# A hybrid mixer and mixture-of-experts layer: the last stage fetches both expert outputs of 64 tokens onto the two halves of the partitions and sums them with two column tiles

## The chip, the core and the metric

The kernel runs on one core of a Trainium2 chip. The metric is the device time in microseconds (us) of one execution. The profile shows one execution; its span runs from the first to the last instruction of the program.

## What is computed

The reference runs one decoder layer on 1,088 tokens of width 1,024 (1,024 of a prompt, 64 of eight samples): four token mixers, an output projection, and a mixture of experts, in which each token picks two of 32 experts. A final RMSNorm gives the output. The part that matters here is the end:

```python
w2 = jax.nn.softmax(v2, axis=-1) * p_top          # two gates of each token
...
out = jnp.einsum('nef,efd->nd', act, w_down)      # gated sum of the two experts' outputs
...
x = x + hier_moe(...)
...
y = rmsnorm(x, g_final)
```

## The kernel before

Tokens stand in nine tiles of 128 rows (the last, tile 8, has 64). The experts run in 28 blocks (`step`); each block gathers its tokens, multiplies, and scatters its ungated output rows into a scratch tensor in HBM, `orow`, where token n has the two rows 2n and 2n+1, one for each choice. Weights of later blocks are loaded meanwhile by the SP queue, in order.

On VectorE (DVE) small pieces of table work hang behind certain blocks, in a dictionary `between` (keys 1 to 10 before). Once the last block is scattered, GpSimd (POOL) raises `moe_done`, and the last stage begins:

- SP issues nine loads at L732, in the order `FINAL = [8, 0, 1, 2, 3, 4, 7, 5, 6]`. Each brings the two output rows of a token, 8 KB that lie together, onto that token's own partition (`opair`). Behind them the same queue issues the nine stores of the result (L559), in the same order, each when `y_done` says so.
- Tiles of `PE_TILES` (0, 2, 4, 5, 6) are summed by TensorE (PE): `own_rows(t)` (L2600) copies x into a pair of PSUM banks by the identity, and four products (L2617) add the choices, with the gates on the diagonals of `dg` as weights. There are four pairs of banks, so the fifth tile waits for the DVE to be done with the first. ScalarE (ACT) builds the ten diagonals at L1169 as soon as the gates are there.
- Tiles of `DVE_TILES` (8, 1, 3, 7) are summed by DVE in two instructions each (`add_experts`, L2082).
- ACT squares and sums each tile and takes the root (L1176 or L749, L1161); DVE inverts it and scales (`final_norm`, L2090 and L2095); SP stores.

The gates are computed by DVE after the last block (L2067 to L2071) and released by `gates_ready`, which PE also uses to know that DVE has left the banks of the last blocks.

Some blocks have two or four experts at a time. There `expert_D` and `expert_GU` write products of 64 or 32 output columns to different partitions of one bank, so that the array is split into column tiles (L2545 and L2506).

Of the kernel before, what the change touches and what calls it, by code (L numbers as in the profile page):

```python
# [23 lines left out]
ALU = mybir.AluOpType  # L24
ACT = mybir.ActivationFunctionType
AX_X = mybir.AxisListType.X

P = 128
D = 1024
# [5 lines left out]
TILES = NT // P + 1  # L35
# [4 lines left out]
NE, NG, EG, FF = 32, 4, 8, 128  # L40
# [30 lines left out]
SPARE = 3  # L71
XG = 4
FINAL = [8, 0, 1, 2, 3, 4, 7, 5, 6]
PE_TILES = [0, 2, 4, 5, 6]
DVE_TILES = [8, 1, 3, 7]
NPAR = 31 + 3 + 4


# [135 lines left out]
def rows(i):  # L214

    return NS if i == LAST else P


def build_layer(nc, a):
    with ExitStack() as ctx:  # L220
        def sb(name, shape, dt=F32):
            return ctx.enter_context(nc.sbuf_tensor("sb_" + name, shape, dt))
# [10 lines left out]
        o_x1 = o_ring + 4 * D * 4  # L233
# [7 lines left out]
        def at(name, shape, offset, dt=F32):  # L241
            return nc.alloc_sbuf_tensor_at("at_" + name, shape, dt, offset=lo + offset)
# [43 lines left out]
        def opair(i):  # L286
            return opair_s[:] if i == LAST else opair_p[:, i, :]
# [18 lines left out]
        ovm = at("ovm", [1, NE], o_sg + 3328)  # L306
        again = at("again", [1, NE + 1], o_w + 14624)
        ovb = at("ovb", [1, 3, OVER], o_sg + 3456)
        dg = at("dg", [P, len(PE_TILES), 2, P], o_x1 + 2 * D * 4)
        xin = at("xin", [P, TILES, D], o_x1)  # L310
        x1 = at("x1", [P, TILES, D], o_mix)
        wk = at("wk", [P, 3, WL], o_w)
# [23 lines left out]
        ident = sb("ident", [P, P])  # L336
        ones = sb("ones", [P, P])
        avg = sb("avg", [P, P])
# [39 lines left out]
        sc = sb("sc", [P, 8])  # L378
        gidx = sb("gidx", [P, 1])
        gates = sb("gates", [P, TILES, 2])  # L380
# [3 lines left out]
        carry = sb("carry", [P, NE])  # L384
        rank = sb("rank", [P, NE])
        rjunk = sb("rjunk", [P, NE])
        rk = sb("rk", [P, 2])
        stage = sb("stage", [P, 3, W])
        rki = sb("rki", [P, 2], I32)
# [6 lines left out]
        gex = flat[:, TILES * 56:TILES * 61].rearrange("p (t n) -> p t n", t=TILES)  # L396
        gsum = flat[:, TILES * 61:TILES * 62]
# [11 lines left out]
        orow = nc.dram_tensor("scratch_out", [2 * NT, D], F32, kind="Internal").ap()  # L409

        s = {n: sem(n) for n in (
            "dve_chain", "act_chain", "pool_chain",
            "const_ready", "ident_ready", "gcol_ready", "scol_ready", "zero_ready",
            "small_in", "ws_in", "late_in", "gain_mix_in", "gain_mix_ready", "ln_d_in",
            "gain_ffn_in", "gain_fin_in", "pw_in", "wsT_masked", "wsb_in",
            "sq_done", "rs_ready", "h_ready", "ht_T", "ht_hi", "ht_lo",
            "hi_ready", "lo_ready", "piece_done", "zf_act", "zf_dve",
            "m_ready", "mf_act", "mf_dve", "uc_ready", "v_stats", "v_rsd",
            "v_ready", "v_out", "px_ready", "pd_ready", "ac_ready", "ua_ready",
# [3 lines left out]
            "t2_done", "h2T_ready", "last_T", "last_h2T", "rows_in", "pads_ready", "gex_in", "gex_out", "m_onehot",  # L423
            "eid_ready", "perm_ready", "ones_ready", "place_ready", "table_added", "cols_ready", "idx_ready", "ov_ready", "xg_zero", "three_gathers",
            "xt_half", "xt_done", "first_hi", "first_lo", "htm_hi", "htm_lo", "w_hi0", "w_hi1", "w_lo0", "w_lo1", "gu_half", "gu_done", "sg_ready", "act_ready", "at_done", "att_ready",
            "d_done", "ob_act", "ob_dve", "moe_done", "gates_ready", "dg_ready", "pair_summed", "y_sum", "y_root", "y_done", "y_out")}
        x_in = [sem(f"x_in{i}") for i in range(TILES)]
        raw_in = [sem(f"raw_in{i}") for i in range(2)]
        wo_in = [sem(f"w_out_in{n}") for n in range(3)]
# [5 lines left out]
        pair_in = [sem(f"pair_in{i}") for i in range(TILES)]  # L435
# [113 lines left out]
        def sum_banks(t):  # L549
            return ps[:, t % 4 * 2:t % 4 * 2 + 2, :]  # L550
# [14 lines left out]
        def _(sp):  # L565
# [58 lines left out]
            for g in range(4):  # L624
                q = g % 2 * 64
# [57 lines left out]
            for i in range(TILES):  # L683
# [6 lines left out]
                if i in (4, 7):  # L690
                    n = i // 3 - 1
# [14 lines left out]
            for w in range(FIX, NE):  # L706
                c = LOADS[w - FIX]
# [20 lines left out]
            sp.wait_ge(s["moe_done"], 1)  # L728
            for i in FINAL:
                n = rows(i)  # L730
                src = orow[2 * i * P:2 * (i * P + n), :].rearrange("(t k) d -> t (k d)", k=2)
                sp.dma_start(opair(i)[0:n, :], src).then_inc(pair_in[i], 16)  # L732
            for at in range(TILES):
# [8 lines left out]
        def _(act):  # L742
            do = Chain(act, s["act_chain"])
            A = nc.scalar.activation
# [84 lines left out]
            for i in range(TILES):  # L829
                n = rows(i)  # L830
# [333 lines left out]

            act.wait_ge(s["gates_ready"], 1)
            for t, i in enumerate(PE_TILES):
                n = rows(i)
                for k in range(2):
                    do(A(dg[0:n, t, k, 0:n], ident[0:n, 0:n], ACT.Copy, scale=gates[0:n, i, k:k + 1]),  # L1169
                       s["dg_ready"])  # L1170
            do(A(acts[:], epsc[:], ACT.Sqrt))
            for i in FINAL:
                if i in PE_TILES:
                    t = PE_TILES.index(i)
                    act.wait_ge(s["pair_summed"], t + 1)
# [198 lines left out]
        def _(dve):  # L1374
            do = Chain(dve, s["dve_chain"])
            v = nc.vector
            stt, tt, ts = v.scalar_tensor_tensor, v.tensor_tensor, v.tensor_scalar
# [41 lines left out]
            for c in range(2):  # L1419
                for h in range(2):  # L1420
                    q = slice(h * 64, h * 64 + 64)
# [52 lines left out]
            for i in range(TILES):  # L1474
                n = rows(i)
                do(v.bn_stats(st6[0:n, i, :], vall[0:n, i, :]))
            for i in range(TILES):
                n = rows(i)
# [5 lines left out]
            for i in range(TILES):  # L1484
                n = rows(i)
# [535 lines left out]
            def overflow_blocks():  # L2021
# [3 lines left out]
                do(v.tensor_copy(ovt[:, OVER:2 * OVER], ovb[:, 2, :]))  # L2025
                do(v.tensor_copy(ovt[:, 2 * OVER:2 * OVER + 1], incl[:, NE - 1:NE]), s["ov_ready"])

            between = {1: expert_order, 2: light_columns, 3: extra_columns, 4: other_columns,
                       6: overflow_counts, 7: overflow_sums, 8: overflow_lists, 9: overflow_experts,
                       10: overflow_blocks}  # L2030

# [31 lines left out]
                                expert_out(i, r, bank=0)  # L2063


            dve.wait_ge(s["gex_out"], 1)
            do(v.tensor_reduce(gsum[:], gex[:, :, 0:NG], AX_X, ALU.add))  # L2067
            do(ts(gates[:, :, 0], gex[:, :, NG], 1.0, None, ALU.add))
            do(tt(gates[:, :, 0], gates[:, :, 0], gsum[:], ALU.mult))
            do(v.reciprocal(gates[:, :, 0], gates[:, :, 0]))  # L2070
            do(tt(gates[:, :, 1], gates[:, :, 0], gex[:, :, NG], ALU.mult), s["gates_ready"])  # L2071


            dve.wait_ge(s["moe_done"], 1)
            dve.wait_ge(s["gain_fin_in"], 16)
            def add_experts(i):

                n = rows(i)
                dve.wait_ge(pair_in[i], 16)
                dve.wait_ge(x_in[i], 48)  # L2080
                for k in range(2):
                    do(stt(x1[0:n, i, :], opair(i)[0:n, k * D:(k + 1) * D],  # L2082
                           gates[0:n, i, k:k + 1], x1[0:n, i, :], ALU.mult, ALU.add),
                       s["y_sum"] if k == 1 else None)
# [16 lines left out]
            final_norm(1)  # L2101
            final_norm(2)
            add_experts(3)
            add_experts(7)
            final_norm(3)
            final_norm(4)
            final_norm(7)
# [5 lines left out]
        def _(pe):  # L2113
# [23 lines left out]
            for h, b in ((0, 6), (1, 7)):  # L2137
                mm = pe.matmul(ps[:, b, :], ones[0:1, :], gain[0:1, h * 512:h * 512 + 512],
                               start=True, stop=True)
# [75 lines left out]
            for c in range(2):  # L2215
                mm = pe.transpose(b[:, c * 64:c * 64 + NPAR], par_rows[0:NPAR, c * P:(c + 1) * P],
                                  ident[0:NPAR, 0:NPAR])
            mm.then_inc(s["m_ready"], 1)
            b = m_open("stc")
            for c in range(2):  # L2220
                for h in range(2):
                    q = (2 * c + h) * 120
                    mm = pe.transpose(b[:, q:q + 120], st_rows[0:120, h, c * P:(c + 1) * P],
                                      ident[0:120, 0:120])
# [3 lines left out]
            for r, n, q in ((2, SB * HP, 0), (3, SB * HA, 240)):  # L2228
                for c in range(2):
                    mm = pe.transpose(b[:, q + c * n:q + (c + 1) * n], st_rows[0:n, r, c * P:(c + 1) * P],  # L2230
                                      ident[0:n, 0:n])
# [3 lines left out]
            for h in range(NG):  # L2235
                mm = pe.transpose(b[:, h * P:(h + 1) * P], ws_rows[:, h, :], ident[:])
# [6 lines left out]
            for i in range(TILES):  # L2243
                n = rows(i)
                b = m_open(f"v{i}")
                for k in range(KC):
                    for hpart, wpart in ((0, 0), (0, 1), (1, 0)):
                        mm = pe.matmul(b[0:n, 0:W].rearrange("p (s c) -> p s c", s=2),  # L2248
                                       hT[:, hpart, k, i * P:i * P + n],
                                       vw[:, :, wpart, k * P:(k + 1) * P],  # L2250
                                       start=(k, hpart, wpart) == (0, 0, 0),
                                       stop=(k, hpart, wpart) == (KC - 1, 1, 0))
# [342 lines left out]
            def own_rows(t):  # L2595

                i = PE_TILES[t]
                pe.wait_ge(x_in[i], 48)
                for h in range(2):
                    pe.matmul(sum_banks(t)[:, h, :], ident[:], x1[:, i, h * 512:(h + 1) * 512],  # L2600
                              start=True, stop=False)

            own_rows(1)
            pe.wait_ge(s["gates_ready"], 1)
            pe.wait_ge(s["dg_ready"], 1)
            for t in (0, 2, 3):
                own_rows(t)
            for t, i in enumerate(PE_TILES):
                if t == 3:
                    pe.wait_ge(s["y_done"], FINAL.index(PE_TILES[0]) + 1)  # L2610
                    own_rows(4)
                pe.wait_ge(pair_in[i], 16)
                pe.wait_ge(s["dg_ready"], 2 * t + 2)
                for h in range(2):
                    for k in range(2):
                        q = k * D + h * 512
                        mm = pe.matmul(sum_banks(t)[:, h, :], dg[:, t, k, :], opair(i)[:, q:q + 512],  # L2617
                                       start=False, stop=k == 1)
                mm.then_inc(s["pair_summed"], 1)


# [29 lines left out]
```

## Time and profile before

| What | us |
|---|---|
| Median of 3 runs | 603.12 (602.17 to 603.79) |
| Profiled execution: its own time | 600.14 |
| Profiled execution: span | 598.4 |
| PE busy in the span | 564.5 (94%) |
| DVE busy | 437.8 (73%) |
| ACT busy | 240.2 (40%) |

The granted clock of the profiled execution is 0.982 of TensorE's full speed on average. The busy shares are averages over stages with different limits; the change touches the last stage, about the last 36 us, and two places in the middle of the expert blocks.

### The profile page before, as it was taken

The page shows a single profiled execution, that of the slowest core. Times are in us where ns is not written, and L with a number is a line of the kernel's source. Part 1 is how long each engine was busy: PE and PEld are TensorE (multiplying, and loading weights), DVE is VectorE, ACT ScalarE, POOL GpSimd, SP SyncE. Part 2 cuts the span into 40 slices and gives each one's busy share as a digit, 9 for nine tenths or more (in the row PEclk, how much of TensorE's full clock was granted, in tenths as well). Part 3 has the DMA queues.
Part 4 walks back from the last instruction along what each step waited for, and adds up shares of the span by engine and source line. Part 5 has one row for each costly group of instructions (what it writes and reads, how often), then busy time and mean ns, then how long its engine had stood idle before and what let it go on. Part 6 is the DMA issues. An engine that isn't in the chain of part 4 may idle for free.

```text
span 598.4 us, 9751 instructions
## 1 busy us (share of the span) xinstructions
PE 564.5 (94%) x3392; PEld 467.9 (78%) x3392; DVE 437.8 (73%) x748; ACT 240.2 (40%) x385; POOL 87.1 (15%) x138
## 2 busy tenths in 40 slices
PE   8899999999999999899999997699999999998685
PEld 6799999998899889788888875588766667885232
DVE  4946997999999976835666658889864457875177
ACT  6752112222122425522222114577444447765434
POOL 4400000200000000000000000422533333521100
PEclk9999999999999999999999999799999999999798
DMA  8751210122010320475525337759999999998599
GB/s 307 157 132 40 70 36 1 36 61 68 19 54 17 135 71 1 142 256 211 211 106 222 130 110 244 247 146 378 409 409 409 388 369 390 403 357 315 185 421 370
DMA packets 54773, 120.16 MB, mean 201 GB/s; under 512 B 10867, under 2 KB 29176, under 8 KB 53625
## 3 DMA queue, kind: packets, MB, share of 16 engines
q1 hardware_dynamic: 47237, 101.10, 47.0%
q0 software_dynamic: 6880, 17.84, 8.3%
q8 instruction: 29, 0.48, 0.3%
q10 hardware_dynamic: 596, 0.50, 0.3%
q14 instruction: 31, 0.25, 0.1%
HBM read 100.29 MB, written 25.80 MB: 211 GB/s over the span
## 4 chain that ended last, share of the span: by engine, by line
PE 39%; DVE 18%; SPq 9%; DMA 9%; issue 3%; ACT 2%; POOL 0%; POOLq 0%; DVEq 0%; ACTq 0%
PE ps L2380 14%; PE ps L2202 9%; SPq L650 8%; DMA at_wlater<-in_expert_w_down 4%; DVE at_mixP L1444 3%; DMA at_opair_p<-scratch_out 2%; PE ps L2545 2%; PE ps L2444 2%; DMA scratch_out<-at_outb,at_sperm 2%; PE ps L2506 2%; PE ps L2617 2%; DVE at_hT L1403 1%; PE ps L2485 1%; DVE at_lnsq L1630 1%; PE ps L2130 1%
## 5 line engine op out<-in xcount | busy, mean ns | idle before, releaser
L2202 PE MATMUL ps<-at_hT,at_ring 128*128 128x384 f32 x936 | 165.5, 333 | 0.0
L2202 PEld LDWEIGHTS ps<-at_hT,at_ring 128*128 128x128 f32 x936 | 155.9, 188 | 5.1 <-issue 5.0
L2380 PE MATMUL ps<-at_hT,at_mring 128*128 128x512 f32 (+1 forms) x432 | 102.7, 393 | 1.9 <-DVE at_mring L1598 1.3
L2380 PEld LDWEIGHTS ps<-at_hT,at_mring 128*128 128x128 f32 (+1 forms) x432 | 77.3, 182 | 21.3 <-DVE at_mring L1598 1.7
L1444 DVE SCALAR_TENSOR_TENSOR at_mixP<-at_uc,at_par,at_mixP 128x1024 f32<-128x1024 f32 x60 | 77.1, 1285 | 2.1
L2520 PE MATMUL ps<-at_whi,at_hTm 128*128 128x256 f32 x176 | 50.8, 289 | 0.0
L2522 PE MATMUL ps<-at_whi,at_hTm_lo 128*128 128x256 f32 x176 | 49.3, 280 | 0.0
L2485 PEld LDWEIGHTS ps<-sb_ident,at_xg 128*128 128x128 f32 x224 | 28.3, 191 | 17.6 <-issue 14.5
L749 ACT ACTIVATE at_wk<-at_x 128x1024 f32<-128x1024 f32 (+1 forms) x13 | 13.8, 1059 | 50.6 <-DVE at_x L1670 44.8
L1886 DVE TENSOR_TENSOR at_hTm_lo<-ps,at_hTm 128x1024 fp32r<-128x1024 f32 x21 | 25.7, 1223 | 10.4 <-ACT at_hTm L1049 10.3
L2520 PEld LDWEIGHTS ps<-at_whi,at_hTm 128*128 128x128 f32 x176 | 33.1, 188 | 0.1
L2522 PEld LDWEIGHTS ps<-at_whi,at_hTm_lo 128*128 128x128 f32 x176 | 33.1, 188 | 0.0
L2485 PE MATMUL ps<-sb_ident,at_xg 128*128 128x128 f32 x224 | 30.4, 279 | 2.6 <-DMA at_xg<-scratch_h,at_gidxs 2.4
L1301 POOL DMA_INDIRECT scratch_out<-at_outb,at_sperm x20 | 19.8, 988 | 68.6 <-DVE at_outb L1874 68.6
L1874 DVE COPY at_outb<-ps 128x512 f32<-128x512 f32 x28 | 19.2, 686 | 13.8 <-PE ps L2545 6.4
L1904 DVE TENSOR_TENSOR at_wfirst_lo<-at_wfirst,at_whi 128x1024 fp32r<-128x1024 f32 x18 | 22.1, 1225 | 8.5 <-ACT at_whi L1068 8.1
L1092 ACT ACTIVATE at_outb<-ps 128x512 f32<-128x512 f32 x28 | 16.7, 598 | 27.2 <-PE ps L2545 17.3
L1286 POOL DMA_INDIRECT at_xg<-scratch_h,at_gperm x20 | 23.2, 1161 | 20.1 <-issue 13.6
L2248 PE MATMUL ps<-at_ring,at_hT 128*128 128x256 f32 (+1 forms) x216 | 25.9, 282 | 0.0
L2248 PEld LDWEIGHTS ps<-at_ring,at_hT 128*128 128x128 f32 (+1 forms) x216 | 25.8, 185 | 0.0
L2545 PE MATMUL ps<-at_wlater,at_actT 128*128 128x512 f32 (+1 forms) x60 | 23.0, 601 | 2.0 <-ACT at_actT L1083 2.0
L1049 ACT ACTIVATE at_hTm<-ps 128x1024 fp32r<-128x1024 f32 x21 | 21.6, 1026 | 7.3 <-PE ps L2485 7.3
(331 smaller groups left out, 955.3 us busy)
## 6 DMA issues: line engine op xcount, KB each, us to landing
at_raw<-in_w_in SPq DMA_DIRECT2D x16, 512.0 KB, 3.9
at_opair_p<-scratch_out SPq DMA_DIRECT2D x8, 1024.0 KB, 13.9
at_wlater<-in_expert_w_gate SPq DMA_DIRECT2D x15, 512.0 KB, 13.1
at_wlater<-in_expert_w_up SPq DMA_DIRECT2D x15, 512.0 KB, 16.4
at_wlater<-in_expert_w_down SPq DMA_DIRECT2D x15, 512.0 KB, 20.6
at_wfirst<-in_expert_w_gate SPq DMA_DIRECT2D x9, 512.0 KB, 11.3
at_wfirst<-in_expert_w_up SPq DMA_DIRECT2D x9, 512.0 KB, 13.8
at_wfirst<-in_expert_w_down SPq DMA_DIRECT2D x9, 512.0 KB, 16.0
```

What stands on the lines that cost most here:

```text
L650: sp.dma_start(wexp(j)[:, m * D:(m + 1) * D], src)\
L1286: g.indirect_dma_start(xg[0:n, b % XG, :], None, hs, bass.IndirectOffsetOnAxis(ap=index[0:n, :], axis=0), bounds_check=last_token, oob_is_ ...
L1444: do(stt(y, x, par[:, c, k:k + 1], y, ALU.mult, ALU.add))
L1886: v.tensor_tensor(hTm_lo[j % 2][:], src, hTm[:, j % 2, :, :].bitcast(F32), ALU.subtract).then_inc(s["htm_lo"], 1)
L1904: v.tensor_tensor(half(wexp_lo(w), h), half(wexp(w), h), whi[h][:].bitcast(F32), ALU.subtract).then_inc(s[f"w_lo{h}"], 1)
L2202: mm = pe.matmul(ps[:, bank + r, 0:t1 - t0], w[:, wpart, k * P:(k + 1) * P], hT[:, hpart, k, t0:t1], start=(m, wpart, hpart) == (0, 0, 0), ...
L2248: mm = pe.matmul(b[0:n, 0:W].rearrange("p (s c) -> p s c", s=2), hT[:, hpart, k, i * P:i * P + n], vw[:, :, wpart, k * P:(k + 1) * P], sta ...
L2380: mm = pe.matmul(ps[0:n, b + r, :], mring[:, 1 - i % 2, mpart, k * P:k * P + n], wo[:, wpart, k, r * 512:(r + 1) * 512], start=(c, mpart, ...
L2485: mm = pe.transpose(rows_psum(b)[:, k // 4, k % 4 * P:(k % 4 + 1) * P], xg[:, j % XG, :].rearrange("p (q k) -> p k q", k=KC)[:, k, :], ide ...
L2520: pe.matmul(out, x, high, start=k == 0, stop=False)
L2522: mm = pe.matmul(out, x_low, high, start=False, stop=k == KC - 1)
L2545: mm = pe.matmul(ps[n, bank + r, :], actT[:, j % 2, n], wexp(w)[:, q:q + 512], start=True, stop=True)
```

## The change

For the six tiles of `PE_TILES` (tile 7 joins them and leaves DVE) the load is made in two pieces. The first choices of the tile's tokens, in two groups of 64 tokens, go to partitions 0 to 63, and the second choices to partitions 64 to 127; a partition holds one row of a token of the first group and one of the second. One piece is 64 partitions by two rows of 4 KB. A weight matrix of 128 by 64, with the first gates on one diagonal and the second gates on the other below it, then sums both choices of 64 tokens in one product; the two groups of tokens go to the two halves of the output partitions.

The gates are computed behind block 12 and laid out in the new form behind block 14. A tiny copy on DVE, `dve_clear`, takes over what `gates_ready` told PE. With six tiles on four pairs of banks, two of them wait for a `y_done`.

```diff
-PE_TILES = [0, 2, 4, 5, 6]
-DVE_TILES = [8, 1, 3, 7]
+PE_TILES = [0, 2, 4, 7, 5, 6]
+DVE_TILES = [8, 1, 3]
...
-        dg = at("dg", [P, len(PE_TILES), 2, P], o_x1 + 2 * D * 4)
+        dg = at("dg", [P, len(PE_TILES), 2, P // 2], o_x1 + 2 * D * 4)
...
+        gates2 = rjunk[:, 0:2 * TILES].rearrange("p (t h) -> p t h", t=TILES)
+        ident2 = avg[:, 0:P // 2]
...
             for i in FINAL:
                 n = rows(i)
+                if i in PE_TILES:
+                    src = orow[2 * i * P:2 * (i + 1) * P, :].rearrange("(h t k) d -> k t h d", h=2, k=2)
+                    for k in range(2):
+                        sp.dma_start(opair(i)[64 * k:64 * k + 64, :].rearrange("t (h d) -> t h d", h=2),
+                                     src[k]).then_inc(pair_in[i], 16)
+                    continue
                 src = orow[2 * i * P:2 * (i * P + n), :].rearrange("(t k) d -> t (k d)", k=2)
                 sp.dma_start(opair(i)[0:n, :], src).then_inc(pair_in[i], 16)
...
             act.wait_ge(s["gates_ready"], 1)
             for t, i in enumerate(PE_TILES):
-                n = rows(i)
-                for k in range(2):
-                    do(A(dg[0:n, t, k, 0:n], ident[0:n, 0:n], ACT.Copy, scale=gates[0:n, i, k:k + 1]),
+                for h in range(2):
+                    do(A(dg[:, t, h, :], ident2, ACT.Copy, scale=gates2[:, i, h:h + 1]),
                        s["dg_ready"])
...
+            def make_gates():
+
+                dve.wait_ge(s["gex_out"], 1)
+                do(v.tensor_reduce(gsum[:], gex[:, :, 0:NG], AX_X, ALU.add))
+                do(ts(gates[:, :, 0], gex[:, :, NG], 1.0, None, ALU.add))
+                do(tt(gates[:, :, 0], gates[:, :, 0], gsum[:], ALU.mult))
+                do(v.reciprocal(gates[:, :, 0], gates[:, :, 0]))
+                do(tt(gates[:, :, 1], gates[:, :, 0], gex[:, :, NG], ALU.mult))
+
+            def stack_gates():
+
+                for h in range(2):
+                    for k in range(2):
+                        do(v.tensor_copy(gates2[64 * k:64 * k + 64, :, h], gates[64 * h:64 * h + 64, :, k]))
+                do(tt(ident2, ident[:, 0:64], ident[:, 64:P], ALU.add), s["gates_ready"])
+
+            between = {12: make_gates, 14: stack_gates, 1: expert_order, 2: light_columns, 3: extra_columns, 4: other_columns,
...
-            dve.wait_ge(s["gex_out"], 1)
-            do(v.tensor_reduce(gsum[:], gex[:, :, 0:NG], AX_X, ALU.add))
-            do(ts(gates[:, :, 0], gex[:, :, NG], 1.0, None, ALU.add))
-            do(tt(gates[:, :, 0], gates[:, :, 0], gsum[:], ALU.mult))
-            do(v.reciprocal(gates[:, :, 0], gates[:, :, 0]))
-            do(tt(gates[:, :, 1], gates[:, :, 0], gex[:, :, NG], ALU.mult), s["gates_ready"])
-
-
+            do(v.tensor_copy(sc[:, 6:7], ones[:, 0:1]), s["dve_clear"])
...
-            add_experts(7)
...
-            pe.wait_ge(s["gates_ready"], 1)
+            pe.wait_ge(s["dve_clear"], 1)
             pe.wait_ge(s["dg_ready"], 1)
             for t in (0, 2, 3):
                 own_rows(t)
             for t, i in enumerate(PE_TILES):
-                if t == 3:
-                    pe.wait_ge(s["y_done"], FINAL.index(PE_TILES[0]) + 1)
-                    own_rows(4)
-                pe.wait_ge(pair_in[i], 16)
+                if t in (2, 3):
+                    pe.wait_ge(s["y_done"], FINAL.index(PE_TILES[t - 2]) + 1)
+                    own_rows(t + 2)
+                pe.wait_ge(pair_in[i], 32)
                 pe.wait_ge(s["dg_ready"], 2 * t + 2)
-                for h in range(2):
-                    for k in range(2):
-                        q = k * D + h * 512
-                        mm = pe.matmul(sum_banks(t)[:, h, :], dg[:, t, k, :], opair(i)[:, q:q + 512],
-                                       start=False, stop=k == 1)
+                for c in range(2):
+                    for h in range(2):
+                        q = h * D + c * 512
+                        mm = pe.matmul(sum_banks(t)[64 * h:64 * h + 64, c, :], dg[:, t, h, :],
+                                       opair(i)[:, q:q + 512], start=False, stop=True)
                 mm.then_inc(s["pair_summed"], 1)
```

## Rows read from the trace of the kernel before

**Rows 1.** The chain that ended last, in order of time: start us, us, what.

```profile
562.26 0.47 SPq L732
...
565.00 14.80 DMA at_opair_p<-scratch_out
...
579.84 3.70 PE ps L2617 x8
583.54 1.72 PE ps L2600 x4
585.26 6.88 PE ps L2617 x16
...
592.22 1.12 ACT at_wk L1176 x2
...
593.97 1.28 DVE at_x L2095
```

**Rows 2.** Windows of the last stage: instructions by engine, granted clock, DMA share, GB/s.

```profile
567.00:586.00 19.00, 16.77 (x39) 6.98 (x39) 15.06 (x16) 8.75 (x19) 0.00 (x0) 1.00 1.01 420
587.50:595.00 7.50, 4.62 (x11) 1.71 (x9) 6.54 (x9) 4.18 (x9) 0.00 (x0) 0.95 1.03 421
...
595.50:596.00 0.50, 0.00 (x0) 0.00 (x0) 0.00 (x0) 0.00 (x0) 0.00 (x0) 0.50 0.09 33
...
597.00:597.50 0.50, 0.00 (x0) 0.00 (x0) 0.00 (x0) 0.00 (x0) 0.00 (x0) 0.50 0.73 295
```

**Rows 3.** Timeline of the SP queue in the last stage: start, us, what.

```profile
562.78 4.07 SPq L732 DMA_DIRECT2D at_opair_p<-scratch_out  x8
572.92 0.51 SPq L559 DMA_DIRECT2D out_y_sample<-at_x  x1
577.08 18.53 SPq L559 DMA_DIRECT2D out_y_prompt<-at_x  x8
```

**Rows 4.** DMA issues: the sample's store and the last store; KB, us to landing.

```profile
out_y_sample<-at_x SPq DMA_DIRECT2D x1, 256.0 KB, 15.0
...
out_y_prompt<-at_x SPq DMA_DIRECT2D x1, 512.0 KB, 2.6
```

**Rows 5.** Instructions on the tile `opair_p`: SP's issues (ns min/median/max, first and last start), and landings.

```profile
L732 SPq DMA_DIRECT2D at_opair_p<-scratch_out x8: 422/432/606, 562.8 to 566.4; - x8
...
DMA to landing us min/median/max: 6.7/13.9/20.8
```

**Rows 6.** Loads onto 64 partitions: tile 8's pairs, and the sample's x.

```profile
at_opair_s<-scratch_out SPq DMA_DIRECT2D x1, 512.0 KB, 4.7
...
at_x<-in_x_sample SPq DMA_DIRECT2D x1, 256.0 KB, 3.5
```

**Rows 7.** Loads onto 128 partitions that began with the queue idle.

```profile
at_x<-in_x_prompt SPq DMA_DIRECT2D x1, 512.0 KB, 3.3
...
at_wlater<-in_expert_w_gate SPq DMA_DIRECT2D x1, 512.0 KB, 3.2
```

**Rows 8.** Windows where a stream of loads begins: tile 8 first, and the kernel's own start.

```profile
563.50:566.50 3.00, 3.00 (x4) 1.23 (x5) 0.00 (x0) 2.77 (x8) 0.00 (x0) 0.50 1.01 243
...
2.00:5.00 3.00, 2.69 (x4) 1.16 (x4) 0.00 (x0) 0.71 (x2) 1.34 (x6) 1.00 0.99 340
```

**Rows 9.** PE timeline, products of 512 columns: whole array, then two column tiles.

```profile
436.93 1.98 PE L2545 MATMUL ps<-at_wlater,at_actT 128*128 128x512 f32 x4
...
443.42 1.94 PE L2545 MATMUL ps<-at_wlater,at_actT 128*64 128x512 f32 x8
```

**Rows 10.** Timeline: DVE behind blocks 12 and 14, the gates, and ACT's diagonals.

```profile
465.83 1.23 DVE L1886 TENSOR_TENSOR at_hTm_lo<-ps,at_hTm 128x1024 fp32r<-128x1024 f32 x1 [1.44 <-ACT at_hTm L1049]
...
478.24 1.23 DVE L1886 TENSOR_TENSOR at_hTm_lo<-ps,at_hTm 128x1024 fp32r<-128x1024 f32 x1 [1.45 <-ACT at_hTm L1049]
...
561.65 0.19 DVE L2067 TENSOR_REDUCE sb_stage<-sb_stage 128x9 f32<-128x36 f32 x1 [4.16 <-issue]
...
562.54 0.17 DVE L2071 TENSOR_TENSOR sb_gates<-sb_gates,sb_stage 128x9 f32<-128x9 f32 x1
562.75 4.30 ACT L1169 ACTIVATE at_dg<-sb_ident,sb_gates 128x128 f32<-128x128 f32 x10 [5.36 <-DVE sb_gates L2071]
```

**Rows 11.** DVE in the last stage: tile 7's and tile 3's sums in one merged row.

```profile
581.73 5.25 DVE L2082 SCALAR_TENSOR_TENSOR at_x<-at_opair_p,sb_gates,at_x 128x1024 f32<-128x1024 f32 x4
```

More of the change, by code:

```diff
@@ L425, in build_layer @@
             "xt_half", "xt_done", "first_hi", "first_lo", "htm_hi", "htm_lo", "w_hi0", "w_hi1", "w_lo0", "w_lo1", "gu_half", "gu_done", "sg_ready", "act_ready", "at_done", "att_ready",
-            "d_done", "ob_act", "ob_dve", "moe_done", "gates_ready", "dg_ready", "pair_summed", "y_sum", "y_root", "y_done", "y_out")}
+            "d_done", "ob_act", "ob_dve", "moe_done", "gates_ready", "dve_clear", "dg_ready", "pair_summed", "y_sum", "y_root", "y_done", "y_out")}
         x_in = [sem(f"x_in{i}") for i in range(TILES)]
@@ L2026, in overflow_blocks @@
                 do(v.tensor_copy(ovt[:, 2 * OVER:2 * OVER + 1], incl[:, NE - 1:NE]), s["ov_ready"])
-            between = {1: expert_order, 2: light_columns, 3: extra_columns, 4: other_columns,
+            def make_gates():
[11 more added lines that the diff above has]
+            between = {12: make_gates, 14: stack_gates, 1: expert_order, 2: light_columns, 3: extra_columns, 4: other_columns,
                        6: overflow_counts, 7: overflow_sums, 8: overflow_lists, 9: overflow_experts,
```

## The prediction

> **What bounds the kernel now.** I began with the chain that ended last [rows 1]. It says that SP starts the last stage at 562.26, that PE waits for a load until 579.84, and that PE then works without a pause until 592.14 (3.70 + 1.72 + 6.88 us); ACT and DVE finish, and DVE's last instruction ends at 595.25. Read alone, it makes PE the bound of the last 15 us.
>
> The windows tell something else [rows 2]. From 567 to 586 the core's 16 DMA engines are busy all the time at 420 GB/s while loads run, and from 587.5 to 595 at 421 GB/s while stores run. The only hole is near 595.5 to 596, where 33 GB/s flow. The stage moves 8.5 MiB in and 4.25 MiB out, 13.37 MB; at 420 GB/s that is 31.8 us, and there are 34 between 563.5 and the end of the traffic at about 597.4 (the last window with traffic is 597 to 597.5, three quarters busy). So the transfers bound this stage, and PE's work lies beside them.
>
> The queue's timeline shows why a tile that is ready early leaves no earlier [rows 3]. All loads are issued by 566.85, and the stores stand behind them in the same queue. The sample's 256 KB are issued at 572.92 and land 15.0 us later, at 587.9, right behind the last load (566.4 + 20.8 = 587.2); the last store needs only 2.6 us [rows 4, 5].
>
> **Removed: PE and DVE work, worth little.** A tile's eight records of products take 3.4 to 3.7 us [rows 1]. Two column tiles already run in this kernel: eight records of 64 output columns take 1.94 us where four of 128 take 1.98 [rows 9], so they run two at a time. The new tile is four products, eight such records, about 1.9 us. DVE loses tile 7's two sums, half of 5.25 us [rows 11]. The last tile lands at 587.2 now; PE would need 1.9 us, ACT with the way to it 1.5 and DVE 1.6, as from 592.14 to 595.25 [rows 1]. Its store could be issued at 592.2 in place of 595.25, 3.0 us sooner. But the stores queue. Of the 8.91 MB of loads 0.73 are in by 566.5 [rows 8] and the rest takes 19.5 us at 420 GB/s, so loads are through at about 586.2, a microsecond before the last one lands. The stores' 4.46 MB take 10.6 us at 421 GB/s, to 596.8 in place of 597.4. That is the hole, closed. I take -0.5.
>
> **Moved: the gates, worth nothing.** Gates cost DVE 1.06 us and the diagonals ACT 4.30 us behind them [rows 10]; both lie in the 4 to 5 us in which tile 8's load is under way. Earlier gates free ACT and PE by about a microsecond, before any pair has landed. Behind blocks 12 and 14 they cost five instructions each, about 1.1 us by the gate's own rows. DVE sits idle 1.44 and 1.45 us there until ACT's next operand is ready [rows 10], so both fit. If that cover failed, what follows are the next block's low parts and then PE; 1 us each, 2 us in all, on work that runs beside a full queue of weights. Price 0, bounds 0 and +2. `dve_clear` replaces `gates_ready` with a signal some 1 us earlier: 0. The two waits on `y_done` in PE ask for tiles 0 and 2, which are normalised well before tiles 4 and 7 land: 0 also. If PE did wait for the second, its own rows for tile 5, 1.7 us, would come late and only tile 7's sum with them.
>
> **Added: 12 pieces of 64 partitions, worth most of it.** The queue issues 15 loads in place of nine. Six more at 0.43 to 0.6 us (4.07 us for eight [rows 3], 0.61 the longest [rows 5]) end at about 569.9, ahead of the first store at 572.92: hidden. Rows of 4 KB in place of 8 KB cost nothing visible: stores have 4 KB rows and flow at 421, loads have 8 KB and flow at 420 [rows 2].
>
> The number of partitions is another matter. Tile 8 is the one load of the stage that goes to 64 of them. Its 512 KB take 4.7 us, against 3.2 and 3.3 us for 512 KB spread over 128 [rows 6, 7]. The 256 KB of the sample, also on 64, take 3.5 us [rows 6]. The difference of the two, 262,144 bytes in 1.2 us, is 218 GB/s: half of what flows in [rows 2]. By that a piece of 512 KB takes 2.4 us in a stream, where it takes 1.25 us at 420 GB/s. Twelve pieces take 28.8 us in place of 15.0: +13.8 us, my upper bound for this term.
>
> For the lower bound I take the windows. In the 3 us in which tile 8 enters, 243 GB/s flow; at the kernel's own start, with loads on 128 partitions, 340 [rows 8]. The difference is 0.29 MB, 0.7 us at 420 GB/s. Twelve times that is +8.4 us. It counts a start in which the engines could read ahead into an empty path, and tile 8 alone, so it is too low for a stream of such pieces. Two further outcomes lie below: successive pieces go to opposite halves, and engines that drift apart would use both halves at once; fully so, the term is 0. I take 1.05 us a piece, nearer the upper end because between pieces that follow each other no empty path is left: 12 x 1.05 = +12.6.
>
> The Trainium skill, in the page SBUF — State Buffer, section on the DMA port swizzle, says that partitions 0 to 63 reach only eight of 16 ports, with 196 GB/s for 1 MiB, and that two DMAs at once to the two halves brought only 6% over one. The trace agrees on the first with its 218 GB/s; no run here shows the second yet. By the page's 6%, an estimate would be 28.8 / 1.06 - 15.0 = +12.2 us. The page DMA: Bandwidth & Descriptors, rules for kernel authors, advises one transfer of 128 partitions in place of two to disjoint halves, which speaks against this change.
>
> **Sum.** 12.6 - 0.5 = +12.1 us. On the profiled execution 600.14 + 12.1 = 612.2, with a span of about 610.5. That execution is 3.0 us under the median of the runs, so the median comes to 603.12 + 12.1 = 615.2. Worked forward as a check: tile 8 is through at 566.0 (landed at 567.0, less the microsecond), tiles 1 and 3 take 2.5 us each, 12 pieces 12 x 2.3 = 27.6, so loads end at 598.6. All stores but the last are ready and take 3.93 MB / 421 = 9.3 us, to 607.9. The last tile has landed at 599.6, its store is issued 5.0 us later, at 604.6, and can start at 605.4 (now 595.3 and 596.0), 2.5 us before its turn. It ends at 609.2, the span 1.0 later at 610.2. Should PE fall to 1.2 GHz in its longer waits, as in the window to 566.5 [rows 8], its last 1.9 us become 3.8, which the 2.5 us cover.
>
> **Rivals.** (A) No penalty by halves: the pieces stream at 420 GB/s, because 4.7 us for tile 8 was the start of a stage and not its partitions. For it: tile 8 was also the first read of fresh scratch rows. Against: 3.5 us for half the bytes, and loads elsewhere that start in 3.2. The term is 0, the change -0.5: 602.6 us, no measurable change. (B) Half a penalty: the engines get out of step and a good part of the pieces overlaps with those of the other half; each costs 0.5 us. 12 x 0.5 - 0.5 = +5.5: 608.6. For it: the window of tile 8 holds 243 GB/s, a start included, where a strict half would hold less than 218 [rows 8]. Against: that window has a buffer's worth of free path at its head, which the later pieces lack. (C) Faster: PE decides the end after all, so that the whole 3.0 us of the last tile's chain are saved, 603.12 - 3.0 = 600.1. This needs pieces at full rate and the last store not to queue. It decides once the stores ahead of it are through by 593, against 595.5 now, where the hole begins [rows 2]. The page TensorEngine Tiling (Array Packing) of the Trainium skill promises column tiling up to twice the speed; the trace agrees with 1.94 us [rows 9], and PE's speed decides only in this rival. (D) The DVE work behind blocks 12 and 14 is not hidden: +2 us on top of the forecast, 617.2.
>
> **Chances and range.** The forecast 0.65, (D) 0.05, (B) 0.14, (A) 0.12, (C) 0.04. What a measurement can tell from no change is 0.3%, 1.8 us. So slower is 0.65 + 0.05 + 0.14 = 0.84, same 0.12, faster 0.04. The range leaves out (A) and (C), 0.16, and reaches down to 607, the lower part of (B), and up to 619: upper bound 13.8 - 0.5 + 2 = 15.3, or 618.4. The likeliest case's own range is 611 (lower bound of the pieces, +7.9) to 617 (the upper, +13.3).
>
> **What the new profile would show.** Right: tile 8's and the pieces' stretch from 566 to about 598 with the DMA share at 1 or over and some 215 to 240 GB/s wherever a PE tile loads, 420 for tiles 1 and 3; pieces landing about 2.3 us apart; PE with waits for each pair and 1.9 us of products; the last store at about 604. Wrong if the flow stays near 420 there: then the loads are through by 587 and rival A holds. Between the two, the spacing of landings gives the price directly. Block times up to 562 unchanged would show the gates hidden; a shift of the stage's start would be (D).

## The result and the profile after

The changed kernel takes 615.25 us (614.01 to 616.69, six runs), the kernel before 602.07 us in the six runs beside them: 1.0225 times as long, 95% interval 1.0207 to 1.0242, or 13.5 us by the ratio (13.2 between the medians). Forecast were 615.2 us and slower.

The profiled execution has a span of 612.2 us, 13.8 more than before. The stage starts where it did: SP issues the first load at 562.07 (562.26 before, [rows 1]). All of the loss lies behind that. The windows show it best; the columns are those of [rows 2].

```profile
574.00:577.00 3.00, 1.45 (x4) 0.00 (x0) 1.08 (x1) 1.41 (x3) 0.00 (x0) 0.70 1.02 210
582.00:599.00 17.00, 12.49 (x36) 3.31 (x32) 8.37 (x10) 5.67 (x12) 0.00 (x0) 0.88 1.03 224
601.00:609.50 8.50, 1.94 (x8) 0.49 (x8) 2.56 (x3) 1.41 (x3) 0.00 (x0) 0.82 1.02 419
```

The DMA engines are busy all the time (share 1.02 and 1.03), but while tiles of PE load only 210 to 224 GB/s flow, where 420 did. Busy does not mean fast: the same bytes keep the engines busy for twice as long. Once the loads are through, the stores run at 419, without the hole that stood near 595.5 before [rows 2].

The timeline of the SP queue, against [rows 3]:

```profile
566.49 9.46 SPq L736 DMA_DIRECT2D at_opair_p<-scratch_out  x8
575.99 3.37 SPq L561 DMA_DIRECT2D out_y_sample<-at_x  x1
580.07 26.60 SPq L561 DMA_DIRECT2D out_y_prompt<-at_x  x8
```

and the instructions on `opair_p`, against [rows 5] (durations in ns, min/median/max):

```profile
L736 SPq DMA_DIRECT2D at_opair_p<-scratch_out x12: 580/614/2754, 562.6 to 573.2; - x12
...
DMA to landing us min/median/max: 7.1/19.7/28.0
```

The last piece is issued at 573.2 and lands 28.0 us later, at 601.2. The last tile landed at 587.2 before. From the first issue of the stage to the last landing the loads take 39.13 us in place of 24.97. PE now waits for the loads before every tile. Its timeline for the two last tiles (start, us, what, and the idle time before it):

```profile
597.04 1.94 PE L2632 MATMUL ps<-at_opair_p,at_dg 128*64 128x512 f32 x8 [2.73 <-DMA at_opair_p<-scratch_out]
...
601.24 1.94 PE L2632 MATMUL ps<-at_opair_p,at_dg 128*64 128x512 f32 x8 [2.26 <-DMA at_opair_p<-scratch_out]
```

The last four tiles take 1.94 us each in place of 3.4 to 3.7 [rows 1], as forecast, and nothing comes of it. The first two took 3.41 and 3.68 us, at a lower clock (below).

The gates moved between the expert blocks can be read on DVE:

```profile
464.71 0.18 DVE L2038 TENSOR_REDUCE sb_stage<-sb_stage 128x9 f32<-128x36 f32 x1
...
465.59 0.20 DVE L2042 TENSOR_TENSOR sb_gates<-sb_gates,sb_stage 128x9 f32<-128x9 f32 x1
466.30 1.23 DVE L1893 TENSOR_TENSOR at_hTm_lo<-ps,at_hTm 128x1024 fp32r<-128x1024 f32 x1 [0.51 <-ACT at_hTm L1057]
...
477.12 0.77 DVE L2048 COPY sb_rjunk<-sb_gates 64x9 f32<-64x9 f32 x4
477.92 0.22 DVE L2049 TENSOR_TENSOR sb_avg<-sb_ident 128x64 f32<-128x64 f32 x1
478.71 1.22 DVE L1893 TENSOR_TENSOR at_hTm_lo<-ps,at_hTm 128x1024 fp32r<-128x1024 f32 x1 [0.56 <-ACT at_hTm L1057]
```

They fill the idle stretch in front of `at_hTm_lo`. Of 1.44 and 1.45 us [rows 10], 0.51 and 0.56 are left, and DVE still waits for ACT afterwards, so it is not the gates that hold `at_hTm_lo` back.

### The profile page after: what moved, and what is told of

Same layout as the page of the kernel before. It is cut to its first block, busy times and chain, and to the rows that moved or that the text cites. A ratio compares the mean times of both kernels' runs of the same rounds, so it can differ in the third digit from the quotient of the medians.

```text
span 612.2 us, 9788 instructions
## 1 busy us (share of the span) xinstructions
PE 562.2 (92%) x3404; PEld 462.9 (76%) x3404; DVE 436.0 (71%) x752; ACT 240.2 (39%) x387; POOL 87.0 (14%) x138
## 4 chain that ended last, share of the span: by engine, by line
PE 36%; DVE 18%; DMA 11%; SPq 9%; issue 4%; ACT 2%; POOL 0%; POOLq 0%; DVEq 0%; ACTq 0%
PE ps L2395 14%; PE ps L2217 8%; SPq L652 7%; DMA at_opair_p<-scratch_out 5%; DMA at_wfirst<-in_expert_w_down 4%; DVE at_mixP L1451 3%; PE ps L2560 2%; PE ps L2459 2%; PE ps L2521 2%; DMA scratch_out<-at_outb,at_sperm 2%; SPq L736 1%; DVE at_hT L1410 1%; PE ps L2500 1%; DVE at_lnsq L1637 1%; PE ps L2145 1%
## 5 line engine op out<-in xcount | busy, mean ns | idle before, releaser
L2395 PEld LDWEIGHTS ps<-at_hT,at_mring 128*128 128x128 f32 (+1 forms) x432 | 77.3, 182 | 21.3 <-DVE at_mring L1605 1.6
L2632 PE MATMUL ps<-at_opair_p,at_dg 128*64 128x512 f32 x48 | 14.8, 750 | 15.4 <-DMA at_opair_p<-scratch_out 15.4
```

The source lines that it names most:

```text
L2395: mm = pe.matmul(ps[0:n, b + r, :], mring[:, 1 - i % 2, mpart, k * P:k * P + n], wo[:, wpart, k, r * 512:(r + 1) * 512], start=(c, mpart, ...
```

## The experiments

The theory is that a load onto partitions of one side (0 to 63, or 64 to 127) moves at half rate. Each experiment is compared with the kernel before, run on the same chip beside it (its medians were 601.1 to 601.8 us).

**The halves alone.** `SPLIT` is the list of tiles whose load is cut.

```diff
+SPLIT = [0, 2, 4, 7, 5, 6]
...
+                if i in SPLIT:
+                    for q in range(2):
+                        sp.dma_start(opair(i)[64 * q:64 * q + 64, :], src[64 * q:64 * q + 64, :])\
+                            .then_inc(pair_in[i], 16)
+                    continue
```

> The kernel before, with one edit: the loads of tiles 0, 2, 4, 7, 5 and 6 are each made in two pieces of 64 partitions (tokens 0 to 63, then 64 to 127, rows of 8 KB as before). Layout, sums and gates stay as they are. Theory, half rate by partitions: 12 pieces at about 1.05 us more each, and the store of the last tile still needs PE's old 3.6 us, so 12.5 to 14 us slower than before, ratio about 1.022. Rival 1, the cost of the change lies in its rows of 4 KB: no change here, ratio 1.000. Rival 2, it lies in the gates moved between the expert blocks or in the compute of the last stage: no change here either.

Measured: 615.25 us, ratio 1.0236 (1.0211 to 1.0261). The edit alone, with 8 KB rows, the old sums and the old gates, makes as much loss as the whole change. Both rivals fall. Windows of this kernel, loads and then stores:

```profile
583.00:598.00 15.00, 10.65 (x18) 3.95 (x17) 9.01 (x10) 5.71 (x12) 0.00 (x0) 0.82 1.01 219
602.00:610.00 8.00, 4.39 (x10) 1.62 (x9) 2.90 (x4) 2.82 (x6) 0.00 (x0) 0.93 1.03 421
```

**As many pieces, on all partitions.**

```diff
+                    for q in range(2):
+                        sp.dma_start(opair(i)[:, q * D:q * D + D], src[:, q * D:q * D + D])\
+                            .then_inc(pair_in[i], 16)
```

> The kernel before, with one edit: the loads of the same six tiles are each made in two pieces of 128 partitions with rows of 4 KB (the first choices, then the second choices). As many pieces, as many bytes in each and the same row size as in the change, but all 128 partitions in each piece. Theory, half rate by partitions: no measurable change, ratio 1.000, within 1 us. Rival, the number of pieces, their issue on the queue or their 4 KB rows: about 13 us slower, ratio 1.022.

Measured: 601.01 us, ratio 0.9998 (0.9981 to 1.0015). Neither the number of pieces nor their rows of 4 KB cost anything that the time shows. The window does show a little: 409 GB/s while only such pieces load, where the kernel before has 422 in its window from 571 to 585.

```profile
577.00:585.00 8.00, 6.64 (x16) 2.61 (x15) 6.60 (x8) 2.38 (x6) 0.00 (x0) 1.00 1.03 409
```

**The gates alone**, computed behind block 12, with the small copy that tells PE about the banks.

```diff
+            between = {12: make_gates, 1: expert_order, ...
...
+            do(v.tensor_copy(sc[:, 6:7], ones[:, 0:1]), s["dve_clear"])
...
-            pe.wait_ge(s["gates_ready"], 1)
+            pe.wait_ge(s["dve_clear"], 1)
```

> The kernel before, with the gates computed behind block 12, and a small copy on DVE that tells PE when the banks are free; the loads and sums of the last stage stay. Theory, the work is hidden in an idle stretch of DVE: within 1 us of before, ratio 1.000. Rival, it delays the expert blocks: 1 to 2 us slower, and the stage's first load issued that much later.

Measured: 601.36 us, ratio 1.0006 (0.9992 to 1.0021). No measurable change. Its profiled execution starts the stage at 563.04 against 562.26, but that start varies between the executions: 561.61 and 561.95 in two of the experiments that leave the blocks alone, 563.31 in a third. The edit has only the gates behind block 12, not their new layout behind block 14.

**A third of the pieces.**

```diff
+SPLIT = [5, 6]
```

> As the first of these experiments, but only tiles 5 and 6 are loaded in pieces of 64 partitions: four pieces instead of 12. Theory, every piece costs the same: a third of the 13.8 us measured with twelve, 4.6 us slower than before, ratio 1.0076. Rival, the loss is a start-up or a one-time effect of the first pieces: well under 2 us, or as much as with twelve.

Measured: 606.08 us, ratio 1.0085 (1.0062 to 1.0107), 5.1 us. Twelve pieces cost 14.2 us, so one costs 1.2 to 1.3 by either. The same queue, in the same execution, first with whole tiles and then with pieces:

```profile
571.00:579.00 8.00, 6.36 (x16) 2.31 (x14) 6.62 (x7) 4.02 (x9) 0.00 (x0) 1.00 1.02 424
582.00:589.00 7.00, 4.42 (x9) 1.75 (x8) 6.75 (x8) 4.30 (x9) 0.00 (x0) 0.86 1.03 221
```

**Number of partitions, or side?**

```diff
+                    for q0, q1 in ((32, 96), (0, 32), (96, 128)):
+                        sp.dma_start(opair(i)[q0:q1, :], src[q0:q1, :]).then_inc(pair_in[i], 16)
```

> The kernel before, with the loads of the same six tiles each in three pieces: partitions 32 to 95, then 0 to 31, then 96 to 127. The first piece has 64 partitions as in the change, but lies across the middle of the partitions. Theory, what counts is on which side of partition 64 a piece lies: the first piece moves at full rate (1.25 us for 512 KB), the two others at half rate (1.2 us each for 256 KB), 3.65 us a tile in place of 2.5, so 6 times 1.15, 7 us slower than before, ratio about 1.011. Rival, every piece of 64 partitions or less moves at half rate: 13.8 us slower, ratio 1.023.

Measured: 610.94 us, ratio 1.0145 (1.0109 to 1.0181), 8.7 us, between the two forecasts and clear of the rival's 1.023.

```profile
583.00:593.00 10.00, 7.47 (x15) 2.58 (x14) 6.13 (x6) 3.44 (x7) 0.00 (x0) 0.92 1.02 265
...
602.50:606.00 3.50, 0.64 (x2) 0.00 (x0) 1.51 (x3) 1.41 (x3) 0.00 (x0) 1.00 0.45 180
```

At 265 GB/s a tile takes 3.96 us, 1.46 more than before; I had worked out 3.65. A tile in these three pieces therefore flows better than one in two halves with as many bytes. That it is the piece across the middle which gains is argued and not shown: the last piece of a tile (96 to 127) and the first of the next (32 to 95, on both sides) can be under way together. The second window shows a new hole: the other stores are through, and the last two wait for PE, which here needs 8.83 us for the sixteen records of the last two tiles, partly at the lower clock (0.59 from 594 to 598):

```profile
594.00:598.00 4.00, 3.69 (x5) 1.65 (x6) 3.86 (x5) 1.34 (x3) 0.00 (x0) 0.59 0.98 378
602.00:608.50 6.50, 1.14 (x3) 0.19 (x1) 2.27 (x3) 1.41 (x3) 0.00 (x0) 0.99 0.51 208
```

From 602 to 608.5 only 208 GB/s flow; at 420 the same bytes would take 3.2 us, so 3.3 us are lost there. That is a loss beside the slow loads. Without column tiles PE's tail does come into view here, once loads are slow and PE has waited for them. The four runs lie between 607.41 and 612.32; the profiled one took 611.31.

**Smaller pieces, the sides in turn.**

```diff
+                    for k in range(2):
+                        for q in range(2):
+                            sp.dma_start(opair(i)[64 * q:64 * q + 64, k * D:k * D + D],
+                                         src[64 * q:64 * q + 64, k * D:k * D + D]).then_inc(pair_in[i], 16)
```

> As the first of these experiments, but with pieces of half the size: 64 partitions by one row of 4 KB, the two sides in turn, four pieces a tile, 24 in all. Theory, the engines pass from one side to the other in step, so that the size of a piece doesn't matter: 12 to 14 us slower than before, as with twelve. Rival, a piece of 256 KB fits into what an engine can have under way, so that both sides work at once: 0 to 5 us slower.

Measured: 612.96 us, ratio 1.0191 (1.0165 to 1.0218), 11.5 us. Below the 12 to 14 expected, far above the rival. The flow is 241 GB/s in place of 219: a finer change of sides gives back about a tenth.

```profile
583.00:598.00 15.00, 9.88 (x20) 4.09 (x19) 10.51 (x12) 5.71 (x12) 0.00 (x0) 0.89 1.03 241
```

**Both sides at once, from two queues.**

```diff
+                    sp.dma_start(opair(i)[0:64, :], src[0:64, :]).then_inc(pair_in[i], 16)
...
+            act.wait_ge(s["moe_done"], 1)
+            for i in FINAL:
+                if i in SPLIT:
+                    ...
+                    act.dma_start(opair(i)[64:P, :], src[64:P, :]).then_inc(pair_in[i], 16)
```

> As the first of these experiments, but the pieces of partitions 64 to 127 are issued by ACT on a queue of its own at the start of the stage, beside SP's, so that loads to both sides are under way at once. Theory, each of the 16 engines serves the two queues in turn and both sides are written at once: most of the loss is gone, 1 to 6 us slower than before. Rival, the engines are in step all the same or the two streams get in each other's way: 12 us or more slower.

Measured: 617.34 us, ratio 1.0283 (1.0249 to 1.0317), 17 us. My expectation was wrong and the rival right. With both queues under way the flow was 252 GB/s, and 207 at the end, when only pieces of SP's side are left:

```profile
568.00:589.00 21.00, 13.74 (x26) 5.75 (x25) 8.16 (x9) 7.81 (x17) 0.00 (x0) 0.78 1.01 252
592.00:599.00 7.00, 4.60 (x7) 2.08 (x8) 5.34 (x5) 1.44 (x3) 0.00 (x0) 0.76 1.02 207
```

The 252 must not be held against the 219 of the halves on one queue: in these 21 us SP's queue also loads tiles 1 and 3 onto all partitions, and with one queue 262 GB/s flow in the same window, as the first line below shows. The second line, of the two queues again, is a stretch in which SP loads a piece of one side, ACT pieces of the other, and nothing else is loaded.

```profile
568.00:589.00 21.00, 12.08 (x23) 4.66 (x22) 10.68 (x12) 7.59 (x15) 0.00 (x0) 0.91 1.01 262
...
580.70:584.20 3.50, 0.00 (x0) 0.00 (x0) 3.40 (x4) 0.92 (x1) 0.00 (x0) 0.50 1.03 269
```

Two sides at once gave 269 GB/s there, and 241 in another such stretch, from 569 to 572.4. What that won was lost again while tiles 1 and 3 shared the engines with ACT's pieces (246 GB/s from 572.8 to 580.3, 250 from 584.6 to 591.8, where these tiles alone flow at 420): from the first issue to the last landing the loads took 39.9 us, against 38.8 in the halves on one queue. The rest of the 17 us is order: tiles complete late and together, PE sums the last two one behind the other, and the last store waits for it (150 GB/s from 611 to 613).

**The change without the halves.** Each partition again has two rows, and the same two column tiles sum them, but with the choice running fastest along the partitions: token t's choices on partitions 2t and 2t+1. PE brings the gates into the new order in block 14.

```diff
-                    src = orow[2 * i * P:2 * (i + 1) * P, :].rearrange("(h t k) d -> k t h d", h=2, k=2)
-                    for k in range(2):
-                        sp.dma_start(opair(i)[64 * k:64 * k + 64, :].rearrange("t (h d) -> t h d", h=2),
-                                     src[k]).then_inc(pair_in[i], 16)
+                    src = orow[2 * i * P:2 * (i + 1) * P, :].rearrange("(h q) d -> q h d", h=2)
+                    sp.dma_start(opair(i).rearrange("q (h d) -> q h d", h=2), src).then_inc(pair_in[i], 16)
...
+                if isinstance(b, int) and b == 14:
+                    pe.wait_ge(s["gates_a"], 1)
+                    for h in range(2):
+                        pe.matmul(ps[:, 2 + j % 2, 256 + 2 * TILES * h:256 + 2 * TILES * (h + 1)],
+                                  rsel[:, h * P:(h + 1) * P],
+                                  gates[:].rearrange("p t k -> p (t k)"), start=True, stop=True)
```

> The changed kernel with another layout of the same data: the choice changes fastest along the partitions (token t's choices stand on partitions 2t and 2t+1), so that one load of 128 partitions with two rows of 4 KB brings a tile. The product of two column tiles, six tiles on PE, early gates and the small copy stay as in the changed kernel; the gates are brought into the new order by two small products in block 14. Theory, half rate by partitions: the whole loss is gone, and the last hole in the transfers is closed: 0 to 1 us faster than before, ratio 0.998 to 1.000. Rival, the loss comes from the compute, the column tiles or the early gates: still 10 us or more slower than before.

Measured: 602.16 us, ratio 1.0016 (1.0000 to 1.0032). The loss is gone but for 0 to 2 us, and so the column tiles, the sixth tile on PE and the early gates had next to no part in it. The gain of 0 to 1 us that I expected of them is not there either; the ratio lies above the 0.998 to 1.000 expected. Windows during the loads, and over the former hole:

```profile
577.00:585.00 8.00, 8.00 (x24) 2.50 (x22) 5.87 (x7) 2.90 (x8) 0.00 (x0) 0.85 1.03 410
595.00:597.00 2.00, 0.00 (x0) 0.00 (x0) 0.00 (x0) 0.00 (x0) 0.00 (x0) 0.50 1.03 420
```

The hole is closed, but the loads with 4 KB rows flow at 410. The 6.3 MB of the six tiles at 410 in place of 422 take 0.45 us more, about what the hole gave back. The profiled stage, from its first issue to the end of the span, is 37.3 us long, against 36.1 before; the loads' landings account for 0.4 of that, and the rest no run separates.

**Tile 8 by itself.** Does its load of 64 partitions cost the kernel before anything? This kernel leaves out the right sum of the sample's tokens and is there for its time alone.

```diff
+                if i == LAST:
+                    sp.dma_start(opair_s[:, 0:D], orow[2 * i * P:2 * (i * P + n), :]).then_inc(pair_in[i], 16)
+                    continue
```

> The kernel before, with tile 8's 128 rows of 4 KB loaded onto 128 partitions, one row each, in place of two rows onto each of 64. The same bytes; the sum for the sample's tokens then takes wrong rows (the first half of the partition twice), which is left as it is. It asks what the one load of 64 partitions costs the kernel before by itself. Theory, a piece of 512 KB on one side costs 1.15 us extra: 0.7 to 1.2 us faster than before, ratio 0.998 to 0.999, and tile 8 lands in about 3.7 us in place of 4.7. Rival, the slow start is that of the stage and not of the 64 partitions: no change, and 4.7 us again.

Measured: 601.06 us, ratio 0.9989 (0.9973 to 1.0005): 0.8 us less by the medians, not clear of no change. The landing is clear, 3.3 us in place of 4.7 [rows 6], with the same bytes at the same place of the program:

```profile
at_opair_s<-scratch_out SPq DMA_DIRECT2D x1, 512.0 KB, 3.3
```

In the profiled execution the last load but one lands 21.3 us after the first issue, where it took 22.5 before: the microsecond is won. Then the flow falls, for a reason that no run shows, and the last load lands 25.1 us after the first issue, as before (25.0):

```profile
584.00:586.00 2.00, 2.00 (x6) 0.95 (x5) 1.96 (x2) 1.94 (x4) 0.00 (x0) 1.00 0.85 246
```

**Tile 8 taken into the interleaved version.**

```diff
-PE_TILES = [0, 2, 4, 7, 5, 6]
+PE_TILES = [8, 0, 2, 4, 7, 5, 6]
```

> The version with both choices interleaved along all 128 partitions, and tile 8 taken into it too: its 128 rows on 128 partitions, its sum on PE as a seventh tile, and no sums of it on DVE. Theory: against the version without tile 8 in it, 1 us faster, about the same as before or up to 0.5 us faster (ratio 0.998 to 1.001). Rival, the stage's start costs the same with any layout: ratio 1.0016 again.

Measured: 602.32 us, ratio 1.0008 (0.9991 to 1.0026). Tile 8 landed in 3.4 us; the time is that of the kernel before. It ran against other executions than the version without it, and the intervals overlap, so the expected microsecond between them is not shown by the times. In the traces it is there in the loads, which take 24.1 us from the first issue to the last landing, against 25.3 in the version without tile 8 in it. But the stage began at 564.37 in this execution, against 562.53, and its stores have a hole, in which DVE, busy for 1.93 of 2 us, is behind with the tiles:

```profile
592.00:594.00 2.00, 1.75 (x10) 0.30 (x6) 1.93 (x3) 1.94 (x5) 0.00 (x0) 1.00 0.72 283
```

No version measured here beats the kernel before.

## Why the prediction was right

**The term of the pieces.** It was sized from two landings on 64 partitions, 262,144 bytes in 1.2 us, 218 GB/s. The experiments show 219 and 221 GB/s for halves with rows of 8 KB. The table has the loss in three ways. By the flow it is 524,288 bytes at the measured rate, less 1.25 us, times the number of such halves (24 quarters are 12 halves; for the pieces across the middle, 1 MiB, less 2.50 us, and six tiles). By the landings it is the time from the stage's first issue to the last landing of a load in the profiled execution, less the 24.97 us of before. By the ratio it is the measured time, known to 1 or 2 us either way.

| Kernel | GB/s in the loads | By the flow, us | By the landings, us | By the ratio, us |
|---|---|---|---|---|
| Changed kernel | 224 | 12 x 1.09 = 13.1, less the hole 0.5 | 14.2, less the hole 0.5 | 13.5 |
| 12 halves | 219 | 12 x 1.14 = 13.7 | 13.9 | 14.2 |
| 4 halves | 221 | 4 x 1.12 = 4.5 | 4.7 | 5.1 |
| 6 tiles in three pieces | 265 | 6 x 1.46 = 8.8 | 9.6 | 8.7 |
| 24 quarters in turn | 241 | 12 x 0.93 = 11.1 | 11.8 | 11.5 |
| 12 pieces of 128 partitions | 409 | 12 x 0.03 = 0.4 | 0.5 | -0.1 |

The three agree within 1.1 us. In the row of the three pieces the agreement is in part luck: the hole in its stores, 3.3 us of transfers where 0.5 stood before, should come on top of the loads, and 8.7 has an interval of 6.6 to 10.9.

I took 1.05 us a piece where the flow gives 1.09 and the landings 1.18. The lower bound, 0.7, was too low, as its reasons said; the upper one, 1.15, was met by the halves with 8 KB rows.

**How much of the hit is luck.** The mechanism was forecast and found. That 615.2 meets 615.25 so closely is luck: the forecast added 12.1 us to a median of 603.12, and measured were 13.5 us on a median of 602.07. The change was 1.4 us larger than forecast, the base a microsecond lower.

**Rival A** (the slow start of tile 8 is the stage's) is refuted by tile 8's 3.3 us on 128 partitions. **Rival B** (engines out of step overlap the two sides) is right in direction and small: 224 in place of 219 GB/s in the changed kernel, 241 with finer pieces, 241 and 269 where two queues load the two sides and nothing else. The Trainium skill (SBUF — State Buffer, "Can I just issue two DMAs to hit both halves?") gives 6% for two DMAs at once, one to each half. On 218 GB/s that would be 231, an estimate. The two queues show more in those stretches, 10% and 23% over 219, and no gain over the whole stream of loads, 39.9 us against 38.8. **Rival C** (PE decides) did not come about: with the full rate restored and the last store ready earlier, no time was gained. **Rival D** (gates delay the blocks): no measurable cost of the gates behind block 12. Those behind block 14 were not run alone; they are seen in DVE's idle stretch.

**The hole.** It closed, -0.5 us as forecast, by the windows; too small for the times to show.

**What was off without harm.** SP's issues were to end at 569.9 and ended at 575.95: a piece took 0.61 us to issue where a tile took 0.43, and the last three took 2.30, 1.04 and 2.75 us. The rows of 4 KB do not explain the 0.61: the two whole tiles between the pieces took 0.60 here, and the pieces with rows of 8 KB in the halves alone 0.60 as well. So the sample's store was issued at 575.99, not at 572.8; it stood behind loads until 600 anyhow. PE's granted clock fell to 0.50, which is 1.2 GHz, at the first two tiles, each time after PE had waited over 4 us for a load (0.50 from 573 to 575, and again from 580 to 581). The prediction allowed for it at the last tile, where it did not come; at the first ones the queue covered it. The last load landed at 601.2 and not at 599.6. Of these 1.6 us 0.5 come from the size of a piece; the rest lies mostly around tiles 1 and 3, which landed 3.8 and 3.5 us behind the piece ahead of them, where 2.5 were worked out, with 1.9 to the piece that follows each, where 2.3 were. That rows of 4 KB cost nothing was slightly wrong: 409 or 410 GB/s against 422. And 19.5 us from 566.5 end at 586.0, not at 586.2, which changes nothing.

**What stays open.** Why two streams to the two sides at once stay at 241 to 269 GB/s, why loads onto all partitions slow down beside pieces of one side on the other queue, and why the pieces across the middle gave 265 and not 287 (1 MiB in the 3.65 us worked out), no run here separates.

## What to carry to other kernels

When a stage is bound by transfers, look at the flow in GB/s beside the DMA share: a share of 1 at half the flow is a loss that no busy number shows. Before laying data on half of the partitions to feed PE better, see whether the same rows can be spread over all partitions with another order (here, the choice running fastest), and price the load first. A faster engine beside a saturated queue brings at most the holes in the queue, half a microsecond here, however many microseconds of its own work it saves.

## What the hardware showed that I had not expected

- Two issuing queues that load the two sides at the same time do not bring the rate back: 241 and 269 GB/s, against 219 for one queue and 420 for loads onto all partitions. Loads onto all partitions that share the engines with pieces of one side lose their rate too: 246 to 250 GB/s in all. Over the stage the second queue won nothing (39.9 us of loads against 38.8).
- A load of 64 partitions across the middle, with two of 32 at the ends, flows at 265 GB/s, better than two halves with as many bytes at 219.
- 256 KB onto 64 partitions land in 3.5 us, 512 KB in 4.7, and 512 KB onto 128 in 3.2 to 3.4 [rows 6, 7]. No run has 256 KB onto 128, so at what size the loss begins is open.
